# An encoder block with product-key experts: gate copies two chunks sooner, a residual's norm and a fold of squares off GpSimd, a last norm on one number per token, and x at the head of the load queue

## What is computed

```python
def rms_norm(x, g):
    y = x * lax.rsqrt(jnp.mean(x * x, axis=-1, keepdims=True) + EPS)
    return y * g

h = rms_norm(x, norm_mix_g)
qa, ka, va, qb, kb, vb, ga, gb = split(h @ w_in)
ya = mixer_windowed_gqa(qa, ka, va, bias_a, sink_a) @ w_oa
yb = mixer_dilated(qb, kb, vb, bias_b) @ w_ob
x = x + (sigmoid(ga) * ya + sigmoid(gb) * yb) @ w_out
h = rms_norm(x, norm_ffn_g)
x = x + peer_ffn(h, peer_wq, peer_keys, peer_u, peer_v)
return rms_norm(x, norm_final_g)

def peer_ffn(t, ...):                       # 8 heads, 128 x 128 = 16384 experts
    sc = queries(t @ w_pq) against sub_keys # two halves of 128 keys per head
    expert_idx, gate = softmax over the best 16 of 16 x 16 pairs
    a = gelu(u[expert_idx] . t)             # one neuron per expert
    return sum((gate * a) * v[expert_idx])
```

## Time and profile before

| | us |
|---|---|
| median of 3 runs | 2155.11 (2154.39 to 2155.17) |
| profiled execution | 2152.65 |
| its span | 2150.8 |
| TensorE busy | 2112.7 |
| VectorE busy | 1589.1 |
| ScalarE busy | 1109.6 |
| GpSimd busy | 509.1 |

### The profile page before, as it was taken

One profiled execution on the slowest core, in us unless ns is written; L12 is line 12 of the kernel. 1 busy time (PEld: TensorE's weight loads), 2 busy tenths in 40 slices (PEclk: granted clock), 3 DMA queues, 4 the chain that ended last, 5 costly groups with the idle time before them and its releaser, 6 DMA issues.

```text
span 2150.8 us, 40816 instructions
## 1 busy us (share of the span) xinstructions
PE 2112.7 (98%) x13474; PEld 1976.5 (92%) x13474; DVE 1589.1 (74%) x2612; ACT 1109.6 (52%) x1863; POOL 509.1 (24%) x387
## 2 busy tenths in 40 slices
PE   7999999999999999999999999999999999999997
PEld 6888888889988999999899999999999999999996
DVE  6555566667777886888688888888777777777775
ACT  5434455446454555555455555555555554555554
POOL 0000000000002000000999999332222220111120
PEclk9999999999999999999999999999999999999999
DMA  7655554445556456666667676899887876777773
GB/s 245 233 188 192 177 166 158 145 156 195 182 190 226 153 176 210 207 213 222 204 222 224 220 225 220 280 315 313 310 287 285 289 287 215 267 268 262 272 242 128
DMA packets 134461, 482.19 MB, mean 224 GB/s; under 512 B 15422, under 2 KB 18238, under 8 KB 134006
## 3 DMA queue, kind: packets, MB, share of 16 engines
q1 hardware_dynamic: 115928, 414.23, 58.2%
q0 software_dynamic: 18432, 67.12, 8.6%
q10 hardware_dynamic: 30, 0.04, 0.0%
HBM read 477.09 MB, written 4.24 MB: 224 GB/s over the span
## 4 chain that ended last, share of the span: by engine, by line
PE 95%; DVE 2%; issue 1%; DMA 1%; POOL 0%; ACT 0%; DVEq 0%; SPq 0%; ACTq 0%; POOLq 0%
PE ps L1626 35%; PE ps L1633 19%; PE ps L1895 19%; PE ps L1899 10%; PE ps L1656 7%; PE ps L1879 2%; DVE lo L1015 1%; PE ps L1732 1%; PE ps L1750 1%; PE ps L1741 0%; DMA raw<-w_down 0%; DMA x_t<-x_t 0%; POOL one_j L604 0%; PE ps L1825 0%; DVE x L1614 0%
## 5 line engine op out<-in xcount | busy, mean ns | idle before, releaser
L1015 DVE TENSOR_TENSOR lo<-raw,hi 128x1024 fp32r<-128x1024 f32 x760 | 941.7, 1240 | 461.6 <-PE ps L1626 146.7
L628 ACT CAST hi<-raw 128x1024 fp32r<-128x1024 f32 x760 | 794.0, 1051 | 358.2 <-DMA raw<-w_down 260.3
L1626 PE MATMUL ps<-move_u,hi 128*128 128x448 f32 x2048 | 452.8, 369 | 0.0
L1895 PE MATMUL ps<-act_now,hi 128*128 128x448 f32 x2048 | 440.6, 366 | 0.4 <-issue 0.4
L1895 PEld LDWEIGHTS ps<-act_now,hi 128*128 128x128 f32 x2048 | 375.0, 188 | 26.9 <-issue 0.7
L1626 PEld LDWEIGHTS ps<-move_u,hi 128*128 128x128 f32 x2048 | 372.2, 189 | 24.9
L1626 PE MATMUL ps<-move,hi 128*128 128x512 f32 x1536 | 379.7, 395 | 10.9 <-ACT hi L628 10.1
L1626 PEld LDWEIGHTS ps<-move,hi 128*128 128x128 f32 x1536 | 281.3, 189 | 64.8 <-issue 10.1
L636 ACT COPY upper<-ps 128x224 f32<-128x224 f32 (+1 forms) x224 | 80.2, 358 | 481.7 <-PE ps L1626 481.7
L604 POOL TENSOR_SCALAR one_j<-iota,j_t,gate_t 128x128 f32<-128x128 f32 x224 | 295.7, 1328 | 8.7 <-ACT j_t L881 7.5
L1899 PEld LDWEIGHTS ps<-act_now,lo 128*128 128x128 f32 x2048 | 250.8, 191 | 9.2 <-DVE lo L1015 2.7
(11 more groups left out here) (203 smaller groups left out, 1639.5 us busy)
## 6 DMA issues: line engine op xcount, KB each, us to landing
raw<-w_u SPq DMA_DIRECT2D x256, 512.0 KB
raw<-w_down SPq DMA_DIRECT2D x256, 512.0 KB
raw<-w_qk SPq DMA_DIRECT2D x68, 512.0 KB
raw<-w_gate SPq DMA_DIRECT2D x64, 512.0 KB
raw<-w_out SPq DMA_DIRECT2D x32, 512.0 KB
raw<-w_pq SPq DMA_DIRECT2D x32, 512.0 KB
raw<-w_v SPq DMA_DIRECT2D x28, 512.0 KB
raw<-w_o SPq DMA_DIRECT2D x24, 512.0 KB
```

The source lines that it names most:

```text
L628: nc.scalar.copy(hi[slot][:], raw[slot][:]).then_inc(hi_ready, 1)
L1015: nc.vector.tensor_tensor(lo[s % LOS][:], raw[s % RAW][:], hi[s % RAW][:].bitcast(F32), ALU.subtract).then_inc(lo_ready, 1)
L1626: ins = nc.tensor.matmul(ps[bank][:, 0:2 * w], hi[slot][:, col:col + P], m, start=begins, stop=ends)
L1895: return nc.tensor.matmul(ps[d][:, 0:2 * TD], hi[s % RAW][:, d * P:(d + 1) * P], act_now[s % ACTS][:], start=begins, stop=ends)
```

## The change

Five places are changed; each does the same arithmetic as before but for rounding.

1. `g_mix` is loaded from ScalarE's queue; x comes first on SyncE's, in five parts (two, two, four, four and four tiles, two parts ahead of the first weight chunk). VectorE makes the rests of tiles 0 to 7 before the first `lo`, and TensorE waits tile by tile.
2. `xr` is made by VectorE, an operation behind the chunk s = 2 of bodies 1 to 4 of pq. `hs4` is made by ScalarE, tile by tile behind the split of that tile. GpSimd does neither.
3. `gate_t` and `j_t` are copied at s = 0 of the body before Spread instead of s = 2, and VectorE's first `one_i` are made at s = 1 instead of s = 3.
4. The fold of the squares goes from GpSimd to VectorE: one operation behind each of the chunks s = 0, 1, 2 of body 61 of 64 in down.
5. The last norm: squares are the stationary side and one column of ones the moving side, so that the sum stands as one number per token (two columns, 128x1 each). 1 / sqrt is made on 128x2. VectorE multiplies the identity by it (`own_rstd`), and TensorE multiplies that with the ones, which gives 128x256 in PSUM again. The multiplication of x2 goes in parts of five, five, four and two tiles. The identity is loaded again into its place during down.

```diff
+Y_PARTS = ((0, 5), (5, 10), (10, 14), (14, 16))
+X_PARTS = ((0, 2), (2, 4), (4, 8), (8, 12), (12, 16))
...
-            sp.dma_start(g_mix[:], A["g_mix"]).then_inc(g_in, 16)
             load_x(0)
+            load_x(1)
             load("qk", 0, 0, first=True)
-            load_x(1)
             load_x(2)
+            load_x(3)
             load("qk", 0, 1, first=True)
-            load_x(3)
+            load_x(4)
...
-            pool.wait_ge(rstd_done, 1)
-            for q in range(4):
-                part = slice(4 * q, 4 * q + 4)
-                nc.gpsimd.tensor_tensor(xr[:, part, :], x1[:, part, :], rstd[:].unsqueeze(1).to_broadcast([P, 4, T]),
-                                        ALU.mult).then_inc(xr_ready, 1)
...
-            pool.wait_ge(x2_sq, 2)
-            for n in (4, 2, 1):
-                nc.gpsimd.tensor_tensor(sq2[:, 0:n, :], sq2[:, 0:n, :], sq2[:, n:2 * n, :], ALU.add).then_inc(sq_folded, 1)
...
+            nc.scalar.dma_start(g_mix[:], A["g_mix"]).then_inc(g_in, 16)
             nc.scalar.preload_act_table(ACT.Sqrt)
...
+                    nc.scalar.activation(hs4[:, k, :].rearrange("p (q t) -> p q t", q=COPIES),
+                                         xr[:, k, TD:T].unsqueeze(1).to_broadcast([P, COPIES, S]), ACT.Copy,
+                                         scale=g_ffn[:, k:k + 1]).then_inc(hs_ready, 1)
...
             def gelu_and_gates(it, s):
                 gelu_kept(it, s)
-                if s == 2:
+                if s == 0:
...
-            for k in range(4):
+            for k in range(8):
                 x_lo(k)
             lo_of(0, 0, 0)
-            for k in range(4, 8):
-                x_lo(k)
...
+                if 1 <= it <= 4 and s == 2:
+                    part = slice(4 * it - 4, 4 * it)
+                    nc.vector.tensor_tensor(xr[:, part, :], x1[:, part, :], rstd[:].unsqueeze(1).to_broadcast([P, 4, T]),
+                                            ALU.mult).then_inc(xr_ready, 1)
...
             def first_ones(it, s):
                 keep_u(it, s)
-                if s == 3:
+                if s == 1:
...
+            def fold_squares(it, s):
+
+                if it == FOLDED and s in (0, 1, 2):
+                    n = 4 >> s
+                    v.wait_ge(x2_sq, 2)
+                    if s:
+                        v.wait_ge(sq_folded, s)
+                    nc.vector.tensor_tensor(sq2[:, 0:n, :], sq2[:, 0:n, :], sq2[:, n:2 * n, :], ALU.add).then_inc(sq_folded, 1)
...
             v.wait_ge(sq_summed, 8)
-            did(nc.vector.tensor_scalar(mean2[:], ps[0][:, 0:T], 1.0 / D, EPS, ALU.mult, ALU.add))
+            for tt in range(TT):
+                did(nc.vector.tensor_scalar(mean2[:, tt:tt + 1], ps[tt][:, 0:1], 1.0 / D, EPS, ALU.mult, ALU.add))
             wait()
             rsqrt_of(mean2[:], work2[:], rstd2[:], 3)
-            v.sem_inc(rstd2_ready, 1)
+            v.wait_ge(ident_again, 16)
+            for tt in range(TT):
+                ins = nc.vector.tensor_scalar(own_rstd[:, tt * P:(tt + 1) * P], ident[:], rstd2[:, tt:tt + 1], None, ALU.mult)
+            ins.then_inc(rstd2_ready, 1)
+            v.wait_ge(rstd2_spread, 1)
...
-                    if s < 2 and n % 4 == 0:
-                        pe.wait_ge(move_ready, 2 * s + n // 4 + 1)
+                    if s < 2:
+                        pe.wait_ge(move_ready, 8 * s + n + 1)
...
-                        pe.wait_ge(hs_ready, 1)
+                        pe.wait_ge(hs_ready, 4 * g + 4)
...
                     pe.wait_ge(x2_ready, KT // 2 + 1)
-                    nc.tensor.matmul(ps[0][:, 0:T], ones[:], sq2[:, 0, :], start=True, stop=False)
+                    pe.wait_ge(x2_ready, KT // 2 + TT)
+                    for tt in range(TT):
+                        nc.tensor.matmul(ps[tt][:, 0:1], sq2[:, 0, tt * P:(tt + 1) * P], ones[:, 0:1], start=True, stop=False)
...
+            pe.wait_ge(rstd2_ready, 1)
+            nc.tensor.matmul(ps[2][:, 0:T], ones[:], own_rstd[:], start=True, stop=True).then_inc(rstd2_spread, 1)
```

More of the change, by code:

```diff
@@ L663, in _ @@
             for k in range(KT):
-                if k % 4 == 0:
-                    a.wait_ge(x_in[k // 4], 16)
+                for q, (first, _) in enumerate(X_PARTS):
+                    if k == first:
+                        a.wait_ge(x_in[q], 16)
                 if k in (4, 8):
```

44 lines of the change are left out of this document (24 added, 20 removed).

## The result

The changed kernel took 2139.25 us (median of 6 runs, 2138.85 to 2142.32) against 2154.28 us for the kernel before in the same comparison (6 runs, 2152.35 to 2155.17). The ratio is 0.9939, with a 95% interval of 0.9928 to 0.9950. Measured again beside the experiments, the same kernel took 2141.33 us (5 runs, 2138.69 to 2142.71) against 2152.65 (13 runs), ratio 0.9950 (0.9937 to 0.9964). So the change makes the kernel 0.5 to 0.6% faster. Single executions of one kernel differ by 3 to 5 us, more than three of the five parts are worth, and the parts are therefore read from traces.

What follows compares the result with a forecast made beforehand. TensorE was busy 98% of the span, so only its waits and lower clock pay. Gains 4.6 + 5.4 + 1.9 + 1.0 + 0.4 = 13.3 us, from the median 2155.11 to 2141.8 us; range 2138.5 to 2146.5.

Steps and rivals of the forecast that it cites:

- pq, 4.6 forecast: Residual's norm in pq: moving products off GpSimd saves TensorE's waits and clock falls, 4.6 us, ends 3.0 and 6.0.
- The gap left of the first wait: In pq near 690: the first lo still stands behind a ranking, so 1.4 us of TensorE's wait stay.
- the waits from a full VectorE: Later chunks of pq: VectorE has little free time, so TensorE waits 0.5, 0.9 and 0.5 us, 1.9 in all.
- the first fall of the clock: In pq behind the first wait: the granted clock drops to 1.2 GHz, counted as a loss of 1.6 us.
- Counted whole: Rival in pq: VectorE is full, moved products cost their whole time, 1.6 us more; 2143.5 to 2144.5, chance 0.09.
- Spread, 5.4 forecast: First rounds of Spread: earlier gate copies let one_j start sooner and TensorE's lows come earlier, 5.4 us, ends 3.5 and 5.6.
- The second round's lead: Spread: GpSimd's next four one_j end at 1027.0, or 1028.7 by the slow price, against TensorE's need at 1028.8.
- The rival that ended slower than before: Spread: GpSimd loses its lead, TensorE waits 0.6 us in each of 28 rounds, 16.8 us; 2158.5, chance 0.04.
- The fold, 1.9 forecast: Squares in down: GpSimd's fold stretches VectorE's lo beside it; moved to VectorE it costs nothing and gains 1.9 us.
- The start, 0.4 forecast: Program start: waiting per tile leaves TensorE one low after the last split instead of four, 0.4 us, ends -1.3 and +1.0.
- The end, 1.0 forecast: Last norm on 128x2: 2.6 to 3.3 instead of 4.5 us, less two costs, net 1.0 us, ends 0.3 and 1.4.
- the wait for the second tile's bank: End of the program: sums of squares wait for one tile more, a cost of 0.3 to 0.4 us.

Runs made afterwards that it cites:

- e1: Changed kernel with the residual's norm and hs4 back on GpSimd: 2146.87 us (9 runs), pq 4.63 us longer.
- e9: Changed kernel with the rankings of pq one chunk later and the last three parts of xr at s = 3: 2158.34 us (8 runs).
- e7: Changed kernel with two more one_j products ahead of GpSimd's loop, their result overwritten: 2140.97 us (4 runs).
- e12: Changed kernel with last-body sums of squares one tile later and, at the start, TensorE's wait for four tiles at once: 2139.05 us (5 runs).
- e10: Changed kernel with each sum of squares one tile later in the last body, sums still one column wide: 2139.68 us (5 runs).
- e4: Changed kernel with the last norm back on 128x256 and four equal output parts: 2140.70 us (4 runs).
- e11: Changed kernel with last norm on 128x256 and equal output parts as before, but keeping the wait for the second tile before the first sum: 2141.32 us (5 runs).
- e6: Changed kernel with only hs4 back on GpSimd, xr staying on VectorE: 2146.69 us (8 runs), pq 4.86 us longer.

## Why the prediction was right

The range (2138.5 to 2146.5) held both medians of the changed kernel, 2139.25 and 2141.33, under the forecast of 2141.8, and the difference of the two profiled executions is 13.45 us where 13.3 was forecast. That the totals meet so closely is in part luck: the five parts come to 12.88 us in the traces, and 0.67 us of the difference stand where no code was changed; the medians differ by 15.03 us in the first comparison and by 11.32 in the second. What bears the account is each part by itself. Point by point:

- **pq, 4.6 forecast, 4.50 and 4.63 measured (before and e1).** The gap left of the first wait was taken at 1.4 and is 1.39; the waits from a full VectorE at 0.5, 0.9 and 0.5, and are 0.61, 0.64 and 0.20. The clock held over 1.39 us in all eleven profiles that have that gap and no GpSimd beside it. The margin was small: behind a gap of 1.78 us it fell in e9. One term stood on a wrong footing, the first fall of the clock as a cost of its own (e1). It made no difference to the sum, as only the end of VectorE's work decides. The Trainium skill, in "Perfetto Trace Analysis", Optimizing Scalar/DVE Operations, names a saturated DVE as a reason to move work off it. Counted whole, as the prediction put that case, the moved products would have left 3.0 of the 4.6; the trace does not bear that out: three of the four products cost 1.45 us together and the first one none.
- **Spread, 5.4 forecast, 5.41 and 5.45 measured.** `one_j` starts at 1009.62 in the changed kernel, which is 1015.1 on the old scale, as forecast, and four take 4.90 us (5.3 forecast). The second round's lead was put at 1.8 us and is 1.56. The rival that ended slower than before asked whether GpSimd's lead is lost in every round; it is not: from the second round on it never falls under 1.53 us in the changed kernel, and with two more products in the way (e7) 0.07 us are left. The price of that rival was put at half of what its own terms give, as there are 56 rounds of two chunks and not 28: 0.6 us in each would be 33.6 us, not 16.8.
- **The fold, 1.9 forecast, 2.02 and 1.72 measured.** At the new place it cost nothing.
- **The start, 0.4 forecast, 0.59 measured**, of which 0.38 is the edit, by the mechanism named: one low instead of four behind the last split (e12).
- **The end, 1.0 forecast, 0.36 and 0.26 measured.** This is the term that was mis-sized. The norm itself gave 1.31 us (from the start of the last two squares to the first multiplication 4.84 us instead of 6.15), at the low end of the forecast's 1.2 to 1.9, and the larger first part took back 0.24 (8.42 us from that multiplication to the end of the program instead of 8.18). But the wait for the second tile's bank was put at 0.3 to 0.4 us and is 0.7, and e10, which avoids it and the later wait of 0.5 us for a square, is 1.06 us better. The spreading matmul took 1.22 us, behind 2.06 us of idle time and at the lower clock, where 0.3 to 1.1 was allowed.
- **What was not seen at all** is the second outcome of the new end: in four of nine profiles the clock falls in the last body, for 2.4 to 3.8 us, though in none of the changed kernel's own two. The table of mean clocks has one such execution among its eleven. Even that often, 3 us in one of eleven, it would take back about the 0.3 us that the fifth part wins; wide sums (e4, e11) showed no fall in the last body, and no mean under 0.997.

Of the versions here e10 has the best case: 2139.68 us beside 2141.33 for the changed kernel in the same comparison, and an end 1.06 us shorter in the trace (e12: 1.08, with the slower start). By their times alone they can't be told from the changed kernel: the scatter overlaps, and the ratio to the kernel before is 0.9939 for e10, e12 and the changed kernel's first comparison alike.

## What to carry to other kernels

A long GpSimd operation was paid for here by whatever VectorE operation with two SBUF inputs met it (`lo`, the split of h2, `act_now`; the ranking, which reads one, took its usual 0.49 us for the first two steps beside it), and through it by everything queued behind; look for it beside the waits of the bounding engine, and move it to where VectorE has slack, or off GpSimd. Before a step is moved on one engine, follow who waits for it in order on the others: the copy of a result that stands ahead of a `hi` made a move by one chunk cost 17 us, some 5 of them by the clock. And where executions of the same code differ by more than an edit is worth, compare the same instruction's start in both traces and not the totals.

## What the hardware showed that was not expected

- The granted clock is not a function of the gap alone. Behind 2.74 us of idle time it fell to 1.2 GHz in one execution and stayed at 2.4 in another (e1); behind 1.78, 3.54 and 3.67 us (e9, e6, e1) it fell only more than a microsecond after the work had begun again; behind 1.39 us (eleven profiles), 1.36 and 1.47 us (e9) it did not fall; and in four of nine profiles it fell in a body where TensorE had stood still twice for 0.7 us. The Trainium skill says in "TensorE: Matmul & The Clock Gate", Part 1, that the monitor runs freely and is not tied to the kernel's start, so that the moment of a change differs from run to run. The pair of before and e1 fits that: the same gap of 2.74 us, one fall and none.
- GpSimd's loop beside VectorE's settled into a lasting pattern: its lead over TensorE in every second round kept 3.76, 2.98 or 2.21 us over some fifty rounds, by where it began.
- A split of 128x224 on VectorE that takes 0.45 us alone took 3.80 us beside one GpSimd product (e6).
